# A decoder block on one core: attention units taken long and short by turns, and the iterations without a gate half spread out

## The reference

```python
h = rms_norm(x, g_pre_mix) * (1 + sc1) + sh1
q, kc, vc, ksl, vsl, kwn, vwn, nsa_g, u, br_g = split(h @ w_in)
o_nsa = nsa_attention(rope(q), compressed k/v, selected k/v, window k/v, nsa_g)   # 8 heads of 64
o_pool = pool_mixer(u, w_pool, pool_scale)
gate_a, gate_b = split(sigmoid(br_g))
merged = gate_a * (o_nsa @ w_br_nsa) + gate_b * (o_pool @ w_br_pool)
x = x + gt1 * rms_norm(merged @ w_out, g_post_mix)
h = rms_norm(x, g_pre_mlp) * (1 + sc2) + sh2
x = x + gt2 * rms_norm(square(relu(h @ w_fc1)) @ w_fc2, g_post_mlp)
```

## Time and profile before

| | us |
|---|---|
| median of 3 runs | 1556.42 (1551.1 to 1562.0) |
| profiled execution | 1554.45 |
| its span | 1552.7 |
| PE busy | 1433.1 (92%) |
| DVE busy | 1087.0 (70%) |
| ACT busy | 637.0 (41%) |
| attention iterations, first score to last o_out | 257.61 to 673.35 |

### The profile page before, as it was taken

The page is one execution under the profiler, slowest core; times in us unless marked ns, Lnnn a source line. Parts: engine busy times, 40 slices in busy tenths (PEclk is TensorE's granted clock), DMA queues, the critical chain, the costliest instruction groups (busy, mean ns, idle before and its releaser), DMA issues. The chain is left out here.

```text
span 1552.7 us, 19468 instructions
## 1 busy us (share of the span) xinstructions
PE 1433.1 (92%) x7206; PEld 1197.4 (77%) x7206; DVE 1087.0 (70%) x1513; ACT 637.0 (41%) x1112; POOL 623.5 (40%) x517
## 2 busy tenths in 40 slices
PE   2997999999999999999999599999999599999995
PEld 2886777887888888888877478888888487878774
DVE  6759835778888888855415895555556569888887
ACT  2533534555655666642225542222223133242332
POOL 3315412233222322212214532222222858888893
PEclk9999998799999999999999899999999799999998
DMA  9388863122111111155444133333335230505005
GB/s 353 70 258 252 232 150 122 50 67 76 53 52 46 53 45 41 32 193 167 141 133 149 41 110 121 109 111 115 112 136 231 81 136 12 206 1 217 1 0 217
DMA packets 123461, 182.08 MB, mean 117 GB/s; under 512 B 18917, under 2 KB 82917, under 8 KB 121319
## 3 DMA queue, kind: packets, MB, share of 16 engines
q1 hardware_dynamic: 118634, 166.19, 33.0%
q0 software_dynamic: 4736, 14.68, 2.7%
HBM read 132.61 MB, written 41.95 MB: 112 GB/s over the span
## 5 line engine op out<-in xcount | busy, mean ns | idle before, releaser
L1941 PE MATMUL ps<-act_hi,a_hi 128*128 128x512 f32 x448 | 192.4, 429 | 1.8 <-DVE a_lo L1420 1.8
L1943 PE MATMUL ps<-act_hi,a_lo 128*128 128x512 f32 x448 | 176.0, 393 | 0.0
L1942 PE MATMUL ps<-act_lo,a_hi 128*128 128x512 f32 x448 | 175.7, 392 | 0.0
L889 POOL TENSOR_TENSOR w1s<-w1s 128x1024 f32<-128x1024 f32 x32 | 77.9, 2435 | 213.5 <-DVE w_lo L1748 170.5
L831 POOL TENSOR_SCALAR ssum<-ssum 128x1 f32<-128x1 f32 (+1 forms) x160 | 42.8, 268 | 283.8 <-ACT p_win L1154 140.6
L1941 PE MATMUL ps<-wr_hi,hr_hi 128*128 128x512 f32 x320 | 128.3, 401 | 25.9 <-DVE wr_lo L1837 25.9
L1346 ACT ACTIVATE hr_hi<-hs 128x2048 fp32r<-128x2048 f32 x28 | 53.6, 1916 | 185.1 <-PE ps L1943 130.8
L1748 DVE TENSOR_TENSOR w_lo<-w1s,w_hi 128x1024 fp32r<-128x1024 f32 x56 | 72.4, 1296 | 80.7 <-ACT w_hi L1267 80.7
L1829 DVE TENSOR_TENSOR hr_lo<-hs,hr_hi 128x2048 fp32r<-128x2048 f32 x28 | 97.5, 3484 | 44.2 <-ACT hr_hi L1346 44.2
L1943 PE MATMUL ps<-wr_hi,hr_lo 128*128 128x512 f32 x320 | 127.4, 398 | 0.0
L1942 PE MATMUL ps<-wr_lo,hr_hi 128*128 128x512 f32 x320 | 127.4, 398 | 0.0
(11 more groups left out here) (271 smaller groups left out, 4013.5 us busy)
## 6 DMA issues: line engine op xcount, KB each, us to landing
ada<-in_w_ada SPq DMA_DIRECT2D x48, 512.0 KB, 5.8
w1s<-in_w_fc SPq DMA_DIRECT2D x32, 512.0 KB, 4.0
h_dram<-hid SPq DMA_DIRECT2D x32, 512.0 KB, 2.8
hs<-h_dram SPq DMA_DIRECT2D x16, 1024.0 KB, 4.9
w2s<-in_w_fc SPq DMA_DIRECT2D x16, 1024.0 KB, 6.2
raw<-in_w_in SPq DMA_DIRECT2D x28, 512.0 KB, 4.2
g_dram<-g_out POOLq DMA_DIRECT2D x32, 256.0 KB, 2.5
mg<-g_dram SPq DMA_DIRECT2D x16, 512.0 KB, 3.8
```

What stands on the lines that cost most here:

```text
L889: pool.tensor_tensor(out[:, :, :], in0[:, :, :], in1[:, :, :], op).then_inc(left_comb, 1)
L1941: pe.matmul(dst, wh, mh, start=start, stop=False)
L1942: pe.matmul(dst, wh, ml, start=False, stop=False)
L1943: return pe.matmul(dst, wl, mh, start=False, stop=stop)
```

## The change

The units are taken in another order: `BLOCK_PAIRS` puts blocks 7 and 0 together, then 6 and 1, 5 and 2, 4 and 3, and within a pair long and short take turns for the four head pairs. The iterations without a gate half are no more 0 to 3 but 6, 14, 22 and 30. Even units are long blocks, odd ones short; the query buffers follow that, and SP loads them two at a time. The compressed scores are made in all 64 columns for every block, since a buffer is no longer used by blocks of growing width. POOL's stores of gate halves 0 and 1 stand ahead of the loop, and the loads of the attention operand wait for the stores of the last four pairs of units.

```diff
-HALF_OF = dict(zip(range(UNITS + 4 - HALVES, UNITS + 1), range(2, HALVES - 1)))
+UNFILLED = (6, 14, 22, 30)
+HALF_OF = dict(zip([it for it in range(UNITS + 1) if it not in UNFILLED], range(2, HALVES - 1)))
...
+BLOCK_PAIRS = ((7, 0), (6, 1), (5, 2), (4, 3))
+UNIT_ORDER = [(c, pair) for both in BLOCK_PAIRS for pair in range(4) for c in both]
+def block_of(u):
+    return UNIT_ORDER[u][0]
+def pair_of(u):
+    return UNIT_ORDER[u][1]
...
 def cmp_width(c):
-    return min(64, (c + 1) * P // CMP_STRIDE)
+    return 64
...
-        def load_q(c):
-            if c == 0:
+        def load_q(n):
+            if n == 0:
...
-            if c >= 2:
-                sp.wait_ge(score_mm, STEPS * 4 * (c - 1))
-            sp.dma_start(full(q_st[:, c % 2, :, :]), q_dram[c]).then_inc(q_in[c % 2], 16)
+            if n >= 2:
+                sp.wait_ge(score_mm, STEPS * (8 * (n // 2) - 1 + n % 2))
+            sp.dma_start(full(q_st[:, n % 2, :, :]), q_dram[BLOCK_PAIRS[n // 2][n % 2]]).then_inc(q_in[n % 2], 16)
...
-            if m % 2 == 1 and m // 2 + 1 < TT and m >= 3:
-                load_q(m // 2 + 1)
+            if m in (7, 10, 14):
+                load_q(2 * (m // 3 - 1))
+                load_q(2 * (m // 3 - 1) + 1)
...
-            for v in (UNITS - 5 + i, UNITS - 4 + i):
+            for v in (UNITS - 8 + 2 * i, UNITS - 7 + 2 * i):
...
+        gate_store(0)
+        gate_store(1)
         for it in range(UNITS + 1):
...
-            if it == 0:
-                gate_store(0)
-                gate_store(1)
...
         def scores(u, s):
-            c, n = u // 4, STEPS * u + s
-            g = (u % 4) // 2
+            c, n = block_of(u), STEPS * u + s
+            g = pair_of(u) // 2
...
-            if s == 0 and u % 4 == 0:
-                pe.wait_ge(q_in[c % 2], 16 * (c // 2 + 1))
+            if s == 0 and u % 8 < 2:
+                pe.wait_ge(q_in[u % 2], 16 * (u // 8 + 1))
```

More of the change, by code:

```diff
@@ L107, in key_tiles @@
     return [(0, j) for j in range(c + 1)] + [(1, j) for j in range(first, c + 1)] + [(2, 0)]
+BLOCK_PAIRS = ((7, 0), (6, 1), (5, 2), (4, 3))
[4 more added lines that the diff above has]
+    return UNIT_ORDER[u][1]
 def n_banks(u):
-    return (len(key_tiles(u // 4)) + 1) // 2
+    return (len(key_tiles(block_of(u))) + 1) // 2
 BANKS_BEFORE = [sum(n_banks(v) for v in range(u)) for u in range(UNITS + 1)]
@@ L855, in _ @@
                 pool.wait_ge(o_sum, v + 1)
-                c, pair = v // 4, v % 4
+                c, pair = UNIT_ORDER[v]
                 pool.dma_start(o_dram[pair * P:(pair + 1) * P, c * P:(c + 1) * P].rearrange("(h d) q -> d h q", h=2),
@@ L1171, in transposed_hi @@
                 act.wait_ge(pv_mm, n - 2)
-            w = 256 * min(2, len(key_tiles(u // 4)) - 2 * b)
+            w = 256 * min(2, len(key_tiles(block_of(u))) - 2 * b)
             act.activation(pt_hi[:, n % 3, 0:w], ps[:, 4 + n % 2, 0:w], ACT.Copy).then_inc(pthi, 1)
@@ L1650, in normalise @@
                 w = cmp_width(c) if s == 4 else sum(q[1] for q in score_parts(c, branch))
-                at = 3 * (2 * (u % 4) + hh) + (1, 2, 0)[branch]
+                at = 3 * (2 * pair_of(u) + hh) + (1, 2, 0)[branch]
                 ins = dve.tensor_scalar(buf[:, u % 2, hh, 0:w], buf[:, u % 2, hh, 0:w], srec[:, n % 4, x:x + 1],
@@ L2090, in scores @@
         def scores(u, s):
-            c, n = u // 4, STEPS * u + s
-            g = (u % 4) // 2
+            c, n = block_of(u), STEPS * u + s
+            g = pair_of(u) // 2
             if n >= 2:
                 pe.wait_ge(exp_done, n - 1)
-            if s == 0 and u % 4 == 0:
-                pe.wait_ge(q_in[c % 2], 16 * (c // 2 + 1))
+            if s == 0 and u % 8 < 2:
+                pe.wait_ge(q_in[u % 2], 16 * (u // 8 + 1))
             base = 2 * (n % 2)
             if s < 4:
-                branch, q = s // 2, q_st[:, c % 2, 2 * (u % 4) + s % 2, :]
+                branch, q = s // 2, q_st[:, u % 2, 2 * pair_of(u) + s % 2, :]
                 parts = score_parts(c, branch)
@@ L2115, in scores @@
                     w = cmp_width(c)
-                    dst, q = ps[:, base, 64 * hh:64 * hh + w], q_st[:, c % 2, 2 * (u % 4) + hh, :]
+                    dst, q = ps[:, base, 64 * hh:64 * hh + w], q_st[:, u % 2, 2 * pair_of(u) + hh, :]
                     pe.matmul(dst, q, kc_hi[:, g, 0:w], start=True, stop=False)
@@ L2122, in transposes @@
         def transposes(u, b):
-            c, n = u // 4, BANKS_BEFORE[u] + b
+            c, n = block_of(u), BANKS_BEFORE[u] + b
             if n >= 2:
@@ L2141, in value_products @@
         def value_products(u, b):
-            c, n, g = u // 4, BANKS_BEFORE[u] + b, (u % 4) // 2
+            c, n, g = block_of(u), BANKS_BEFORE[u] + b, pair_of(u) // 2
             pe.wait_ge(ptlo, n + 1)
```

## The result

The changed kernel takes **1571.78 us** (median of 4 runs, 1570.01 to 1578.06); the kernel before took 1556.14 beside it (4 runs). The ratio is 1.0106, with a 95% interval of 1.0061 to 1.0152. I had forecast 1558 with a range of 1546 to 1572 and "no change" as the likeliest: the kernel is slower by 1.1%, at the upper end of the range and on the side to which I gave a chance of 0.08. The profiled execution took 1570.01 us.

The account below looks back on a forecast made before the run. PE was taken to bound the kernel nearly everywhere, DVE second. Opening -21.8, unfilled iterations +16.4 and clock +6.8 summed to +1.4 us; 1556.42 + 1.4 was rounded to 1558 us, range 1546 to 1572.

Parts of the forecast that it names:

- no change: Whole kernel: time within 1% (15.6 us) of the kernel before, chance 0.87; slower by over 1%, 0.08.
- Opening, -21.8: Opening iterations without a gate half: 21.8 us lost to waits and clock are won back; iterations 0 to 3 without idle PE.
- The unfilled iterations: Iterations 6, 14, 22, 30: DVE's chain outlasts PE's work, restarts at 10.0 to 11.0 us; together 16.4 us lost, bounds 0 to 24.
- at the low level its scores still fit between DVE's steps: Iteration 6: even at the low clock, PE's scores fit between DVE's steps; the clock comes back only in the filled iteration behind.
- I book 0 for the 29 filled iterations: Filled iterations: PE leads DVE, 11.7 against 10.6 us in long ones, 13.2 against about 9 in short ones; loss 0.
- the short iteration lets DVE catch up: Filled pairs: a lag of DVE is made good in the short iteration, 13.2 us on PE and about 9 on DVE.
- The clock, 6.8: Unfilled iterations and those behind: the clock falls, about 1.7 us lost four times, 6.8 us; bounds 0 and 10.
- The rival by which the clock holds: Unfilled iterations: the clock does not fall in some or all, up to 6.8 us less, 1551; chance 0.17.
- Moved queues, 0: SP's query and raw loads: they land in time behind their new waits, no cost.
- Slacker than the chain: Unfilled iterations: slacker than the DVE chain, as iterations 1 to 3 were; +8, 1566; chance 0.18.
- DVE becomes the bound in the long filled iterations: Long filled iterations: over 11.7 us on DVE, PE stalls in each of 12; 26 to 32 us, about 1585; chance 0.06.
- the prediction's own signs of being wrong: PE waits in filled long iterations, the clock dips are missing, or an unfilled iteration takes under 9 or over 12.5 us.

Follow-up runs that it names:

- e2: Kernel before with only the iterations without a gate half moved to 6, 14, 22 and 30, old unit order kept: 1559.12 us, ratio 1.0022.
- e5: Changed kernel with the 24 products of the gate half before repeated, unused, in iterations 6, 14, 22 and 30: 1571.31 us, ratio 1.0114.
- e3: Changed kernel with POOL's and ACT's splits of gate blocks only in the short iterations: 1567.05 us, ratio 1.0073.
- e7: Changed kernel with two gate halves shared over three iterations around each hole, and splits moved to short iterations: 1554.41 us, ratio 0.9997.
- e1: New unit order alone, iterations without a gate half still 0 to 3 as in the kernel before: 1562.10 us, ratio 1.0044.
- e4: Changed kernel with the iterations without a gate half moved to the short ones 7, 15, 23 and 31: 1561.56 us, ratio 1.0040.
- e8: Kernel before, old unit order, with seven of eight parts of a gate half in each of iterations 0 to 31: 1545.57 us, ratio 0.9931.
- e6: Changed kernel with two gate halves shared over three iterations (4, 8 and 4 parts) around each hole: 1558.55 us, one run.

## Why the prediction was wrong, point by point

The forecast for the stage was +1.4 us; measured +16.5. At full clock the stage holds 415.7 - 21.8 = 393.9 us of PE's work, so the changed stage loses 38.3, where the prediction had 16.4 + 6.8 = 23.2. By the prediction's terms the 38.3 are 22.7 in the holes, 4.1 by the clock behind them and 11.5 in the filled iterations.

- **Opening, -21.8: right in kind.** Iterations 0 to 3 run at clock 1.00. e2 wins most of it (17.1) in the old order. That iteration 0 would hold no idle PE was wrong: it holds 1.58 us, counted with the filled iterations below.
- **"The unfilled iterations", 16.4: mis-sized, 22.7 measured** (48.3 us from first score to first score, less 25.6 of work). By iteration 1.9, 0.7, 2.6 and 1.0 us too short. The links were right, their starts were not. Timeline of the changed kernel in iteration 6, DVE and PE:

```profile
332.63 0.39 PE L2121 MATMUL ps<-k_hi,q_st 128*128 128x512 f32 x1
...
333.95 0.42 DVE L1699 TENSOR_TENSOR o_out<-ps,o_tmp 64x256 f32<-64x256 f32 x1 [0.73 <-ACT o_tmp L1218]
334.29 1.21 DVE L1646 TENSOR_REDUCE smax<-ps 128x1 f32<-128x1024 f32 x1
...
339.79 0.42 DVE L1636 TENSOR_TENSOR pt_lo<-ps,pt_hi 128x256 fp32r<-128x256 f32 x1 [0.63 <-ACT pt_hi L1189]
...
342.54 0.82 DVE L1646 TENSOR_REDUCE smax<-ps 128x1 f32<-128x640 f32 x1 [0.48 <-PE ps L2127]
...
344.53 0.58 PE L2121 MATMUL ps<-k_hi,q_st 128*128 128x256 f32 x1 [1.06 <-ACT p_win L1170]
```

  PE begins the iteration's scores at 332.63 and DVE its first maximum at 334.29, 1.66 us later, not 0.8: the compressed step and o_out of the unit before stand ahead on DVE. I had followed DVE alone and booked ACT as always ready; the pt_lo waits 0.63 us for an ACT that is behind its exponential. The fourth maximum waits 0.48 for its scores, at a clock of 0.83; "at the low level its scores still fit between DVE's steps" failed there. These three, 0.86 + 0.63 + 0.48, come to about the 1.9 us of iteration 6; the other three holes I have not followed link by link. e5 shows that the chain, not PE, sets the length.
- **"I book 0 for the 29 filled iterations": failed, 11.5 measured** (38.3 - 22.7 - 4.1). This is the step that put the total furthest off. About 4.7 of it (e3's 6.2 less the 1.5 of iteration 7) is the split in the long iterations, POOL's holding DVE's normalise above all, shown by e3. I had the row (635.71 in the earlier trace rows, 1.29 against 0.81), put it with a rival at 0.06, and said that the short iteration lets DVE catch up. It can't: PE has already waited inside the long one, 0.87 us in iteration 2. A lag is made good only if the bound engine has work queued that does not need it. What remains, about 7 us, is open. It lies in part in long iterations of the middle blocks (0.6 of idle PE in e3's iteration 18, behind ACT), in part in PE's work itself, which the prices put too low for the new pairs: e3's iterations 2 and 3 take 11.93 + 13.38 = 25.3 us with PE idle for 0.13, where I had 11.7 + 13.2 = 24.9.
- **The clock, 6.8: too much, 4.1 measured** (2.8 in iteration 7, 1.3 in 15, against 13.3 at full clock). Behind the holes 22 and 30 it was 1.00, though it had sunk within 22 (0.87). The rival by which the clock holds would have given 1551; the clock held throughout at one hole of four and cost nothing behind two, and the time went up for other reasons. That the 4.1 came out under the 6.8 was no merit of the estimate, which had all four alike. Of the two rules of the Trainium skill, "TensorE: Matmul & The Clock Gate", the one in section "HAM oscillation — how this bites in real kernels", which counts only idle gaps beyond a length that it names, does not fit: the clock fell in iteration 6, whose longest gap was 2.0 us, shorter than that. The other, in section "A second HAM failure mode: psum-queue depth-cycling", on short and frequent idling, fits the falls but does not say when they come: iteration 30, with PE idle for 3.3 of 12.0 us, kept 1.00.
- **Moved queues, 0: right.** No load is among PE's waits here. The cover was thin, though: e7 has two late query loads, 1.1 us together.
- **Rivals.** "Slacker than the chain" (+8, 1566) is the nearest: +6.3 on that term. "DVE becomes the bound in the long filled iterations" was right in its place and mechanism and too dear: 4.7 us rather than 26 to 32, since the clock never fell in a filled long iteration. Each was given alone; both happened at once: 1.4 + 6.3 + 4.7 - 2.7 and the 7 us that stay open make the 16.5. Two of the prediction's own signs of being wrong came: PE waits in filled long iterations, and an unfilled one took over 12.5 us (22). e1 and e2 give the same total from the other side: 9.0 for the order, 2.2 for the spread, and 5 more for the two together. That these 5 arise because the spread holes land on the long iterations that the order makes fits e4, but no run shows it alone.
- **The range.** The measured 1571.78 lies just within its upper end (1572), by luck: that end was made of slack holes and a dear clock, not of the filled iterations.

## What to carry over

Filler work in a software-pipelined loop is worth only what the iteration's own dependency chain leaves free: before moving it, compare each iteration's chain (here DVE and ACT, 11 to 13 us in the long ones) with its length, and leave gaps where the chain is short, or spread them as thinly as possible, as e8 does. Two iterations of unequal chain don't average out, since the engine that waits has waited by the time the slack comes. When two rivals act on different terms, add them up before setting the upper end.

## What the runs showed of the hardware

- A DVE multiplication by a scalar within SBUF, 0.81 us at 128x1024, took 2.61 when it started behind a running POOL subtraction of 2.40 us, and ended 0.55 after it; a 128-wide one took 1.32 (e3) instead of 0.35, and ended 0.09 after it. DVE's pt_lo, with one input in PSUM, was not held in the same stretch: 0.69 us at 298.70 in e3, with POOL's subtraction from 298.33 on.
- The clock behind the same hole is not the same every time: 0.81 after iteration 6, 0.88 after 14, 1.00 after 22 and 30, and e4 (e6 too) had 0.89 in an iteration 1 that ran at 1.00 in the changed kernel behind the same iteration 0 (10.16 us busy of 11.73 and 11.74). What decides it stays open.
